# Turning q and k for a layer's attention: from TensorE and PSUM to VectorE blocks and a trip through DRAM

## The reference

```python
h = _rmsnorm(x, norm_g)
proj = h @ w_in
qa, ka, va, za, qb, kb, vb, zb, fb, qm, zm, gl = _split_cols(proj, IN_WIDTHS)
qa = _rmsnorm(qa.reshape(B, S, 12, 128), q_norm_a)     # the same for ka, and for branches b, m
oa = _dilated_mixture(qa, ka, va, rel_bias)            # logits q.k / sqrt(d) + bias, softmax, @ v
ob = _forgetting_attention(qb, kb, vb, log_f)          # 8 heads of 128
om = _memory_attention(qm, km, vm)                     # 4 heads of 256; km, vm = rmsnorm(mem) @ w_mem_kv
ua = (oa * silu(za)) @ w_proj_a                        # the same for b and m
x = x + (g0 * ua + g1 * ub + g2 * um) @ w_out
```

## Time and profile before

| | |
|---|---|
| Median of three runs | 1215.76 us (1215.35 to 1215.8) |
| The profiled execution: its own time | 1215.12 us |
| Its span in the trace | 1213.3 us |
| TensorE, weight loads | busy 99%, 83% |
| VectorE, ScalarE, GpSimd | busy 56%, 44%, 3% |
| Loads and stores | 235 MB, 16 DMA engines busy about 59% |

### The profile page before, as it was taken

The page is one execution under the profiler, slowest core; times in us unless marked ns, Lnnn a source line. Parts: engine busy times, 40 slices in busy tenths (PEclk is TensorE's granted clock), DMA queues, the critical chain, the costliest instruction groups (busy, mean ns, idle before and its releaser), DMA issues.

```text
span 1213.3 us, 14994 instructions
## 1 busy us (share of the span) xinstructions
PE 1205.5 (99%) x5596; PEld 1003.1 (83%) x5596; DVE 681.2 (56%) x871; ACT 535.4 (44%) x672; POOL 35.1 (3%) x22
## 2 busy tenths in 40 slices
PE   8999999999999999999999999999999999999998
PEld 7888888888888888888888888888888888888887
DVE  6656554555556565565565555565556555555643
ACT  5654444434534534444444453434435443443432
POOL 0000000010000000000000000000000000000000
PEclk9999999999999999999999999999999999999999
DMA  9667555555565564564564564467557546755761
GB/s 329 209 198 270 195 194 175 196 171 177 174 200 173 173 209 163 173 206 166 183 203 161 187 205 160 165 205 236 182 176 229 202 156 225 212 194 196 272 211 49
DMA packets 121459, 235.40 MB, mean 194 GB/s; under 512 B 7575, under 2 KB 11852, under 8 KB 120908
## 3 DMA queue, kind: packets, MB, share of 16 engines
q1 hardware_dynamic: 108592, 218.44, 54.1%
q10 hardware_dynamic: 12828, 16.42, 4.6%
HBM read 231.16 MB, written 6.06 MB: 196 GB/s over the span
## 4 chain that ended last, share of the span: by engine, by line
PE 98%; DMA 1%; DVE 0%; ACT 0%; SPq 0%; issue 0%; DVEq 0%
PE acc L970 30%; PE acc L972 30%; PE acc L971 30%; PE side L993 2%; DMA w_raw<-in_x_dram 1%; PE side L1010 1%; PE side L1034 1%; PE side L1006 1%; PE side L1024 1%; DMA w_raw<-in_w_in_dram 1%; PE side L1044 0%; PE side L1042 0%; PE side L1040 0%; PE side L1011 0%; PE side L1099 0%; PE side L1069 0%
## 5 line engine op out<-in xcount | busy, mean ns | idle before, releaser
L610 DVE TENSOR_TENSOR w_lo<-w_raw,w_hi 128x1024 fp32r<-128x1024 f32 x408 | 498.5, 1225 | 482.9 <-ACT w_hi L340 482.8
L340 ACT ACTIVATE w_hi<-w_raw 128x1024 fp32r<-128x1024 f32 x408 | 431.0, 1061 | 603.2 <-PE acc L972 590.6
L970 PE MATMUL acc<-w_hi,hT_hi 128*128 128x512 f32 x1152 | 454.1, 394 | 0.9 <-DVE hT_lo L632 0.6
L972 PE MATMUL acc<-w_hi,hT_lo 128*128 128x512 f32 x1152 | 449.0, 390 | 0.0
L971 PE MATMUL acc<-w_lo,hT_hi 128*128 128x512 f32 x1152 | 448.3, 389 | 0.0
L970 PEld LDWEIGHTS acc<-w_hi,hT_hi 128*128 128x128 f32 x1152 | 216.4, 188 | 45.3 <-DVE w_lo L610 0.7
L972 PEld LDWEIGHTS acc<-w_hi,hT_lo 128*128 128x128 f32 x1152 | 216.2, 188 | 45.5
L971 PEld LDWEIGHTS acc<-w_lo,hT_hi 128*128 128x128 f32 x1152 | 216.5, 188 | 43.3
L970 PE MATMUL acc<-w_hi,mT_hi 128*128 128x512 f32 x256 | 101.1, 395 | 0.0
L972 PE MATMUL acc<-w_hi,mT_lo 128*128 128x512 f32 x256 | 99.8, 390 | 0.0
L971 PE MATMUL acc<-w_lo,mT_hi 128*128 128x512 f32 x256 | 99.7, 389 | 0.0
(11 more groups left out here) (138 smaller groups left out, 549.8 us busy)
## 6 DMA issues: line engine op xcount, KB each, us to landing
w_raw<-in_w_in_dram SPq DMA_DIRECT2D x143, 1024.0 KB, 5.0
w_raw<-in_w_mem_kv_dram SPq DMA_DIRECT2D x16, 1024.0 KB, 6.1
w_raw<-in_w_out_dram SPq DMA_DIRECT2D x16, 1024.0 KB, 5.1
w_raw<-in_w_proj_a_dram SPq DMA_DIRECT2D x12, 1024.0 KB, 5.0
w_raw<-in_w_proj_m_dram SPq DMA_DIRECT2D x8, 1024.0 KB, 5.0
w_raw<-in_w_proj_b_dram SPq DMA_DIRECT2D x8, 1024.0 KB, 5.1
group<-bias_tiles ACTq DMA_DIRECT2D x5, 768.0 KB, 4.2
group<-in_b_gate_dram ACTq DMA_DIRECT2D x12, 256.0 KB, 5.9
```

What stands on the lines that cost most here:

```text
L340: act.activation(whi[:, s % RING], raw[:, slot, UK * (s % 2):UK * (s % 2) + UK], ACT.Copy)\
L610: dve.tensor_tensor(wlo[:, s % RING], raw[:, (s // 2) % RING, UK * (s % 2):UK * (s % 2) + UK], whi[:, s % RING].bitcast(F32), ALU.subtract ...
L970: pe.matmul(banks[t][:], hi, whi[:, s % RING, j], start=first and j == 0, stop=False)
L972: return pe.matmul(banks[t][:], lo, whi[:, s % RING, j], start=False, stop=last and j == UK - 1)
```

## The change

`qn` is no longer transposed by TensorE. VectorE transposes it in 32x32 blocks, in one instruction for each of q and k (`turn`, at s = 15 and 23), into the place of `bias`. There partition 32i+p holds what belongs to partition 32j+p of the transposed matrix. Four stores on SyncE's queue, one for each 32 partitions, write it to DRAM (`turn_write`, 128 KB each, in runs of 1 KB), and one load brings it back with the partitions in order (`turn_read`, 512 KB): q again to the place of `bias`, k straight to its place as `kT`. ScalarE copies q from there to `qT` in one pass, at s = 22, with the product of both gains as its scale (`scale_q`; k needs none then). The load of `bias` moves from s = 11 to s = 28. `kT` now lies in runs of 32 tokens, 1 KB apart. What is computed stays the same.

```diff
-S_QT, S_KT = 15, 23
-U_EVAC = (18, 26)
+U_TURN = (15, 23)
+U_SCALE = 22
+U_BIAS = 28
+L_TURN = (11, 15)
...
-    kT = part(1024, 1024).rearrange("p (b s) -> p b s", b=4)
+    kT = part(1024, 1024).rearrange("p (i t b s) -> p t b i s", i=4, t=TT, b=4)
+    squares32 = part(5120 + 4 * SEG, 1024)
...
+            def turn_write(norm, w):
+                sp.wait_ge(turned, norm + 1)
+                for i in range(4):
+                    rows = slice(32 * i, 32 * i + 32)
+                    sp.dma_start(turn_dram[w][:, i].rearrange("(j p) n -> p j n", j=4),
+                                 squares32[rows].rearrange("p (j n) -> p j n", j=4)).then_inc(turn_out, 16)
+            def turn_read(g, norm, w):
+                sp.wait_ge(turn_out, 64 * norm + 64)
...
+                sp.dma_start((squares32, part(1024, 1024))[w], turn_dram[w].rearrange("p i n -> p (i n)"))\
+                  .then_inc((qT_in, kT_in)[w], 16)
+            def body(kind, g, b, u0, before):
+                def beside(i):
+                    if i == L_TURN[0]:
+                        turn_write(2 * g, 0)
+                    if i == L_TURN[0] + 1:
+                        turn_read(g, 2 * g, 0)
+                    if i == L_TURN[1]:
+                        turn_write(2 * g + 1, 1)
+                        turn_read(g, 2 * g + 1, 1)
...
                 if s == 27:
                     act.wait_ge(pre["crow_out"], 16)
+                    act.wait_ge(turn_out, 64 * 2)
...
-            def evac(kind, norm, which, bank, g):
+            def scale_q(kind, g):
+                act.wait_ge(qT_in, 16 * g + 16)
...
+                    o = act.activation(blocks, landed, ACT.Copy, scale=gcur[:])
+                o.then_inc(q_scaled, 1)
...
+            def turn(g, norm, w):
+                dve.wait_ge(chunk_taken, 8 * g + 2 * w + 2)
...
+                if w:
+                    dve.wait_ge(q_scaled, g + 1)
+                dve.transpose(squares32.rearrange("p (j n s) -> p n j s", j=4, s=32),
+                              qn.rearrange("p t (b j s) -> p (t b) j s", b=4, j=4)).then_inc(turned, 1)
...
             def scores(kind, a, step):
-                pe.wait_ge(qkT_evac, 4 * a + 4)
+                pe.wait_ge(q_scaled, a + 1)
+                pe.wait_ge(kT_in, 16 * a + 16)
...
-                    for i in range(2):
-                        if s == (S_QT, S_KT)[i]:
-                            pe.wait_ge(chunk_taken, 8 * g + 2 * i + 2)
-                            if attn is not None:
-                                pe.wait_ge(probT_copied, 2 * g)
-                            if i or attn is not None:
-                                pe.wait_ge(qkT_evac, 4 * g + 2 * i)
-                            transposes(side[2:4], qn, qkT_done)
```

More of the change, by code:

```diff
@@ L182, in hybrid_block @@
     bias_dram = nc.dram_tensor("bias_tiles", (AB_GROUPS, P, 4, SEG), F32, kind="Internal").ap()
+    turn_dram = [nc.dram_tensor(f"turned_{n}", (P, 4, 256), F32, kind="Internal").ap() for n in "qk"]
     acc = [[nc.alloc_psum_tensor(f"acc{c}{t}", [P, CW], F32) for t in range(TT)] for c in range(2)]
@@ L204, in hybrid_block @@
     squares, sums, means, roots = sem("squares"), sem("sums"), sem("means"), sem("roots")
-    qkT_done, qkT_evac = sem("qkT_done"), sem("qkT_evac")
+    turned, turn_out = sem("turned"), sem("turn_out")
+    qT_in, kT_in, q_scaled = sem("qT_in"), sem("kT_in"), sem("q_scaled")
     z_tanh, gains_set = sem("z_tanh"), sem("gains_set")
@@ L247, in load, with loads @@
                 sp.dma_start(raw[:, slot], view[:, k:k + LK, bass.ds(col, CW)]).then_inc(load_in[slot], 16)
-            def loads(chunks, u0, before):
+            def loads(chunks, u0, before, beside=None):
                 i = 0
@@ L278, in loads @@
                             sp.dma_start(cst[:, P:], consts[:, P:]).then_inc(cst_in, 16)
+                        if beside is not None:
+                            beside(i)
                         i += 1
-            def body(kind, b, u0, before):
-                loads([(w, c, KT) for w, c in body_chunks(kind, b)], u0, before)
+            def turn_write(norm, w):
[6 more added lines that the diff above has]
+                sp.wait_ge(turn_out, 64 * norm + 64)
+                if w and fixed(g, 0):
+                    sp.wait_ge(pre["mTp"], 8)
+                    sp.wait_ge(pre["summ"], TT)
+                elif w:
+                    sp.wait_ge(scores_done, 2 * g)
+                sp.dma_start((squares32, part(1024, 1024))[w], turn_dram[w].rearrange("p i n -> p (i n)"))\
[9 more added lines that the diff above has]
+                        turn_read(g, 2 * g + 1, 1)
+                loads([(w, c, KT) for w, c in body_chunks(kind, b)], u0, before, beside)
             for b in range(M_GROUPS):
-                body("m", b, b * BODY_U, None if b == 0 else 2 * CU)
+                body("m", b, b, b * BODY_U, None if b == 0 else 2 * CU)
             ab0 = M_GROUPS * BODY_U
-            body("a", 0, ab0, 2 * CU)
+            body("a", M_GROUPS, 0, ab0, 2 * CU)
             with sp.Fori(1, A_GROUPS) as b:
-                body("a", b, ab0 + b * BODY_U, 2 * CU)
+                body("a", b + M_GROUPS, b, ab0 + b * BODY_U, 2 * CU)
             with sp.Fori(A_GROUPS, AB_GROUPS) as b:
-                body("b", b, ab0 + b * BODY_U, 2 * CU)
+                body("b", b + M_GROUPS, b, ab0 + b * BODY_U, 2 * CU)
             def merge(n, first, u0, before):
@@ L435, in square @@
                 else:
-                    act.wait_ge(qkT_done, 2 * norm)
+                    act.wait_ge(turned, norm)
                 r = t + (TT if kind == "m" and w else 0)
@@ L447, in z_post @@
                 act.activation(silz[:, t], acc[1][t][:], ACT.Tanh, scale=hrx[:, t:t + 1]).then_inc(z_tanh, 1)
-            def evac(kind, norm, which, bank, g):
-                dst = (qT, kT)[which]
-                act.wait_ge(qkT_done, 2 * norm + bank + 1)
-                if not fixed(g, 0):
+            def scale_q(kind, g):
+                act.wait_ge(qT_in, 16 * g + 16)
+                act.wait_ge(pre["gains"], 1)
+                if fixed(g, 0):
+                    act.wait_ge(pre["mTp"], 8)
+                    act.wait_ge(pre["summ"], TT)
+                else:
                     act.wait_ge(scores_done, 2 * g)
[L455 to L458, removed]
+                landed = squares32.rearrange("p (i n s) -> p n i s", i=4, s=32)
+                blocks = part(0, 1024).rearrange("p (n i s) -> p n i s", i=4, s=32)
                 if kind == "m":
                     for i in range(2):
-                        o = act.activation(dst[:, 2 * bank + i], ps[:, i * S:(i + 1) * S], ACT.Copy,
-                                           scale=(gq, gk)[which][:, AB_GROUPS + i:AB_GROUPS + i + 1])
+                        o = act.activation(blocks[:, i::2], landed[:, i::2], ACT.Copy,
+                                           scale=gq[:, AB_GROUPS + i:AB_GROUPS + i + 1])
                 else:
                     act.wait_ge(gains_set, g + 1 - M_GROUPS)
-                    o = act.activation(dst[:, 2 * bank:2 * bank + 2], ps[:], ACT.Copy,
-                                       scale=gcur[:, which:which + 1])
-                o.then_inc(qkT_evac, 1)
+                    o = act.activation(blocks, landed, ACT.Copy, scale=gcur[:])
+                o.then_inc(q_scaled, 1)
             def exps(kind, a, step):
@@ L520, in body @@
                                 square(kind, w, 4 * g + w, 2 * g + w, t)
-                            if s == U_EVAC[w] + t:
-                                evac(kind, 2 * g + w, w, t, g)
-                    if attn is not None and kind == "ab" and s == 11:
+                    if s == U_SCALE:
+                        scale_q(kind, g)
+                    if attn is not None and kind == "ab" and s == U_BIAS:
+                        act.wait_ge(turn_out, 64 * (2 * g + 2))
                         if not fixed(b, 0):
@@ L853, in body @@
                                 normalise(kind, 2 * g + w, w, t)
+                        if s == U_TURN[w]:
+                            turn(g, 2 * g + w, w)
                     if s in U_V:
@@ L1005, in scores @@
                         for i in range(2):
-                            o = pe.matmul(side[step][:, t * S:(t + 1) * S], qT[:, 2 * step + i, t * P:(t + 1) * P],
-                                          kT[:, 2 * step + i], start=i == 0, stop=i == 1)
+                            o = pe.matmul(side[step][:, t * S:(t + 1) * S], qT[:, t, 2 * step + i],
+                                          kT[:, :, 2 * step + i], start=i == 0, stop=i == 1)
                 else:
                     for h in (2 * step, 2 * step + 1):
-                        pe.matmul(side[h][:, 0:S], qT[:, h, P:S], kT[:, h], start=True, stop=True)
-                        o = pe.matmul(side[h][:, S:SEG], qT[:, h, 0:P], kT[:, h, 0:P], start=True, stop=True)
```

(2 more changed lines are left out.)

24 lines of the change are left out of this document (14 added, 10 removed).

## The result

The changed kernel takes 1205.01 us (median of four runs, 1204.53 to 1205.57) against 1215.78 for the kernel before beside it: a ratio of 0.9912, 95% interval 0.9899 to 0.9924. The time lies in the range given, 1.5 us above the forecast of 1203.5. It lies outside the 1202.5 to 1204.5 to which I had given 0.78, and in the 1204.5 to 1206.5 of the first rival, a wait in the first group, to which I had given 0.12. The profiled execution took 1204.53 us, with a span of 1202.5.

What follows compares the result with a forecast made beforehand. TensorE's instruction list was taken to bound the kernel: 1215.12 - 12.3 for removed blocks + 0 for VectorE, trips and logits = 1202.8, or 1203.5 against the median of the runs. The range was 1202.3 to 1206.8 us.

Steps and rivals of the forecast that it cites:

- the first rival: First group: same gain less a 1 to 3 us stall before unit 31 for the forget sums; 1204.5 to 1206.5, chance 0.12.
- What bounds the kernel, and the price of a block: TensorE's instruction list is the time; 14 removed blocks of eight q and k transposes at 0.88 us save 12.3 us.
- The cover: VectorE's added block transposes, 1.3 us each, are hidden by its lead over TensorE: cost 0 up to some 7 us.
- The trip of q: q's stores and load through DRAM end before ScalarE needs it, with 8 us to spare in the fifth group: cost 0.
- The limit of 26 us: Longest time from VectorE's end to q's landing, ScalarE's lead included, before the trip of q costs anything.
- The trip of k: k's trip makes the next group's load 0 about 1 us late, with 10 us to spare: cost 0.
- The first group: Forget sums share DMA with k's load and load 0, landing between 99 and 104; cost 0, bounds 0 to 3 us.
- The other rivals: A late trip of q, chance 0.06, and logits slowed by reading kT in runs, chance 0.04.
- The late trip of q: ScalarE waits for q at s = 22, each us beyond 26 costing 7; 1210.5 to 1231.5, chance 0.06.
- my 59 us: By the skill's 19-times rule for transposing DMA, a 3.1 us store would take 59, stalling every group over 30 us.
- that rival: Logits reading kT in runs 1.6 times as slow take 12.3 us more, leaving the time at 1215.8; chance 0.04.

Runs made afterwards that it cites:

- e8_q_later: Changed kernel with first-group k loaded behind the next group's load 2, and q loaded behind load 14, twice, the second after the first landed: 1222.98 us.
- e5_turn_x5: Changed kernel with first-group k loaded behind the next group's load 2, and from the second group each VectorE block transpose issued five times: 1203.62 us.
- e1_late_k: Changed kernel, but in the first group SyncE waits for k's stores and loads k only behind load 2 of the next group: 1205.04 us.
- e11_late_k_again: Rerun beside the changed kernel of the version that waits for first-group k's stores and loads k behind the next group's load 2: 1203.70 us.

## Why the prediction was right, and where it was short

*What bounds the kernel, and the price of a block.* Right. Twelve blocks between the first logits and the last block of transposes took that stretch from 1132.53 - 115.80 = 1016.73 us to 1121.70 - 115.92 = 1005.78, that is 0.91 each, and the two of the first group are worth 1.73 where no stall hides them. So 12.7 us in place of 12.3. The reading by the chain stands: 273 ns a transpose would have made 30.6 us, and the 275 ns of the Trainium skill (TensorE: Matmul & The Clock Gate, Part 4: PE-mode transpose), which stand there beside a figure for bf16, are a duration, not a price; doubling the blocks added 1.75 us for 16 transposes, 0.109 each, by the periods.

*VectorE.* 1.24 us, forecast 1.3. The cover was forecast at up to some 7 us for k: five transposes in a row (6.4 us) cost nothing, eight (10.2 us) made TensorE wait for what goes beyond 7.7, 2.4 to 2.6 us.

*The trip of q.* Forecast: loaded from DRAM 4.7 us after VectorE was done, there after 12.2. In the profile the load goes out 449.23 - 442.84 = 6.4 us after it, as the four stores take longer (4.6 us to landing in the median, forecast 3.1), and needs 5.7 us (7.5 forecast): 12.1. That 12.1 meets 12.2 is luck, since the two errors cancel. The limit of 26 us was measured to be 26. The wide margin made the stores' length harmless.

*The trip of k.* Load 0 of the next group was forecast to be about 1 us late; it went out at 474.03, 1.6 us behind the `lo` of s = 25 (471.24 + 1.23). Nothing came of it.

*The first group.* Here a term of the sum was mis-sized: I took 0 and gave 0 to 3 us as bounds. Measured are 1.6 us in the first profile and 2.4 in another, and that is the first rival, which I had given 0.12. The mechanism was put rightly, and what travels beside the forget sums wrongly: I reckoned "now 1 MB of theirs shares the engines with 1.5 MB" and came to a landing between 99 and 104. It was 105.1, 11.8 us after the issue. There were not 1.5 MB beside them but 3.5: besides k's load (92.39) and load 0 (92.78), loads 1 and 2 went out at 95.19 and 100.63. I had left these two out, though they come at the same distance from the product at s = 13 (35.4 and 40.8 us) in the kernels without a stall as well. Load 0 was late by 2 us, not by the 4 forecast (33.0 us behind that product, 30.9 before). The DMA issues from 92 to 106 (KB each, median us to landing):

```profile
w_raw<-in_w_in_dram SPq DMA_DIRECT2D x3, 1024.0 KB, 7.7
group<-forget_sums ACTq DMA_DIRECT2D x2, 512.0 KB, 10.4
group<-turned_k SPq DMA_DIRECT2D x1, 512.0 KB, 4.0
```

*The other rivals.* The late trip of q did not happen, and neither rule of the Trainium skill against the change (VectorE: DVE Perf Modes, Rules for kernel authors and The three transpose paths) decided here. The first prefers TensorE for 128x128; here, where TensorE's list is the time, leaving TensorE gained 12.7 us. The second compares a DMA that transposes by large strides between elements with the chip's own DMA transpose, not with a plain store, so my 59 us did not follow from it; the stores, in pieces of 1 KB, landed in 2.3 to 7.7 us and the loads in 3.4 to 9.9. The logits read `kT` at the old pace: 0.43 and 0.22 us for the two products (starts at 497.15, 497.58, 497.80; before at 504.30, 504.73, 504.95). The price of that rival had a slip: 20 x 0.62 is 12.4, not 12.3.

*The account.* 1215.12 - 12.7 (blocks) + 1.6 (stall) + 0.3 (a later start, 59.80 against 59.53) = 1204.3, for a profiled execution of 1204.53. The 0.2 left over lie outside the span: 1204.53 - 1202.5 = 2.0 us against 1.8 before.

## What to carry to other kernels

Where one engine's list is the time, take work off that list even at the price of much more work elsewhere, and price it by the distance between starts in the chain, not by an instruction's duration. Before it, write down for each new trip the last moment at which it may end; here 26 us for q and 7.7 for VectorE, both confirmed, while the one loss came where I had counted only the loads that go out at that moment and not the ones that follow. Behind such a moment look also at what else stands in the waiting engine's queue: q 1.0 us late in the first group cost 4.1, since the forget sums went out behind it. A transfer that nobody needs soon (k's, wanted 20 us later) should be issued behind the one that somebody does.

## What was unexpected in the hardware

- A wait of TensorE of 2.4 to 2.6 us was followed by some 3 us at 1.2 GHz in five cases of six, which cost 1.3 to 1.6 us more than the wait itself. Waits of 0.8 to 1.5 us in the groups of the other kernels were not followed by it, the one of 4.8 us in the first group of `e8_q_later` was. Length alone does not decide: of the waits for the first input at the start of the kernel, one of 1.9 us (`e5_turn_x5`) and one of 2.2 (`e1_late_k`) were followed by it, one of 2.0 (`e11_late_k_again`) was not.
- In the crowded stretch of the first group the transfers suffered unequally: the forget sums on ScalarE's queue, in pieces of 1 KB, went from 4.4 to 10.4 us, k's load on SyncE's queue, in pieces of 4 KB, took 4.0. Whether it is the queue, the size of the pieces or that k's load went out first (92.39 against 92.92 and 93.34) was not tried; behind load 2, in `e1_late_k`, k's load took 6.6 us. The load of `bias`, also on ScalarE's queue, went from 4.2 to 7.0 us, hidden, but it had moved from s = 11 to s = 28, and without any trip it took 6.3 there.
- VectorE transposes 128x1024 float32 in blocks in the time of a plain pass over as many elements (1.24 against 1.23 us).
